# Gates and turned projections of a two-block fp32 kernel as one 512-column product, its bank halves added by ScalarE and VectorE

## The chip, the cores and the metric

The kernel runs on one core of one Trainium2 chip. The metric is the device time of one execution in microseconds (us): the median of several executions. TensorE (PE in the profile) multiplies, VectorE (DVE), ScalarE (ACT) and GpSimd (POOL) do the rest, and SyncE (SP) issues the transfers. Each engine takes its own instructions strictly in the order in which they were issued, and engines meet only in semaphores.

## What is computed

Two transformer blocks over one sequence of 256 rows of 1024 values, in fp32, each with two layers. What matters here is the middle of a layer, cut from the reference of block 2 (block 1 has the same form with three mixers, gmlp, retention and NSA, and a bias in the gates):

```python
u = rms_norm_2(x, norm_mix_g[layer])
proj = jnp.einsum('bsd,de->bse', u, w_in[layer])
(a_in, bq, bk, bv, cq, ck, cv, co, cgate, dq, dk, dv, gates) = split_cols(proj)
y_a = fourier_mix(a_in)
y_b = gqa_branch(bq, bk, bv, qk_norm_g[layer], cos, sin)
y_c = mlstm_branch(cq, ck, cv, co, cgate, mlstm_gate_bias[layer], mlstm_norm_g[layer])
y_d = diff_branch(dq, dk, dv, diff_lambda[layer], diff_norm_g[layer], rel_bias, layer + 1)
ys = jnp.stack([y_a, y_b, y_c, y_d], axis=2)
branch = jnp.einsum('bsnc,ncd->bsnd', ys, w_branch[layer])
g = jax.nn.sigmoid(gates.reshape(b, s, N_BRANCHES, D_MODEL))
merged = jnp.sum(g * branch, axis=2)
x = x + merged @ w_out[layer]
```

Around the middles stand the feed-forward parts (two in a layer of block 1, one with a convolution in a layer of block 2).

## The kernel before

**Precision.** Every fp32 product is three products of rounded parts: hi by hi, hi by lo, lo by hi (`three_passes`, L394 to L396). The normalised input lies turned (features on the partitions) in two tiles, `hT_hi` and `hT_lo`, of 8 chunks (`KC`, index `c`) of 128 partitions by 256 columns.

**Weights.** They stream through a ring of five slots, in tiles of 128 x 2048 values: SP loads a slot, ACT makes its hi part (`hi_to`, L198), DVE its lo part (`lo_to`, L206), and PE uses it and signals it free. A tile of a middle holds 256 output features, that is two halves of 128.

**The middles.** `Fill` (L670 to L831) holds the projections, gates and branch products of a middle as a list of *units*, each half a tile and mostly 24 matmuls of 256 columns. A mixer takes some of them at fixed places of its own code (`f.tensor(pe, n)`), so that PE has work while the mixer's DVE or ACT steps run, and sets a named mark there; ACT and DVE catch up with the units at places of theirs (`f.scalar(act, name)`, `f.vector(dve, name)`). Units are numbered here from 0 in each middle, as u20 for the unit with index 20. Roles: "N" is a projection with the tokens on the partitions, "T" and "half" a turned one (features on the partitions), "gate" a gate half, "branch" a branch product. Turned ones are in Middle1 `uT`, `rqT`, `rkT`, `kcvcT` (u20, u21), `nqT` (u22 to u25) and `kskwT` (u28, u29), 16 halves in all beside 24 gate halves; in Middle2 `aT`, `gt`, `cqT`, `ckT`, `dqT`, `dkT`, 21 halves beside 32 gate halves.

**Banks.** Units are collected in *groups*: one for a whole projection tile (its two halves stand side by side in the bank), one for each gate half or branch half. Group g uses PSUM bank 6 + g % 2, and its first product waits until group g - 2 is read. Before the change ACT reads projections and gates (`activate`, with Copy, Gelu, Silu or Tanh straight from the bank), and DVE only the branch products (`combine`). After the last half of a tile ACT issues the hi part of the tile five ahead, DVE the lo part of the tile four ahead.

**Order.** All orders are fixed in the code; nothing is scheduled at run time. What follows a unit on DVE is what the mixer's code puts there: in the retention mixer (`Retention.vector`, lines before L1082) DVE does the statistics and layer norm of `a_ret_y` (L1061 to L1079) and only then `f.vector(dve, "ret_y")`, the catching up with u22 to u25. PE meanwhile does these four units (L1041), then transposes `a_ret_y` (L642).

Of the kernel before, what the change touches and what calls it, by code (L numbers as in the profile page):

```python
# [9 lines left out]
F32R = mybir.dt.float32r  # L10
# [113 lines left out]
class Core:  # L124


    def __init__(self, nc, ctx):
# [5 lines left out]
        self.hT_hi = sb("hT_hi", [P, KC, SEQ], F32R)  # L133
        self.hT_lo = sb("hT_lo", [P, KC, SEQ], F32R)
# [535 lines left out]
class Fill:  # L670
# [3 lines left out]

    def __init__(self, k, ph, n0, norm, roles, branches, half_bias, gate, mix, ys):
# [21 lines left out]
        self.units[1:3] = self.units[2:0:-1]  # L697
        self.act_out, self.dve_out, self.gated, self.taken, self.mixed = (ph.sem(n) for n in (
            "f_act_out", "f_dve_out", "f_gated", "f_taken", "f_mixed"))
        self.tmp = ph.sb("f_tmp", [P, 2, SEQ])  # L700
        self.out_of, self.mix_at, self.gate_at, self.proj_out = {}, {}, {}, {}
        counts = {"act": 0, "dve": 0, "gate": 0, "taken": 0, "mix": 0}
        sems = {"act": self.act_out, "dve": self.dve_out, "gate": self.gated, "taken": self.taken, "mix": self.mixed}
        for u, (n, h, last, group, role) in enumerate(self.units):
            if not last and role[0] not in ("gate", "branch"):
                continue
# [45 lines left out]
    def product(self, pe, u):  # L752
# [1879 lines left out]
```

## Time and profile before

| | |
|---|---|
| time before, median of 3 runs | 2455.48 us (2451.62 to 2455.94) |
| the profiled execution: its own time | 2453.13 us |
| its span in the trace | 2451.4 us |
| PE busy | 2414.5 us, 98% |
| DVE busy | 1392.6 us, 57% |
| ACT busy | 1138.8 us, 46% |

The share is of the span. The span is the stretch between the first and the last recorded instruction; 1.7 us of the execution lie around it. The profile is of one execution, so differences are made against its own time.

### The profile page before, as it was taken

What the parts mean: (1) busy time and instruction counts of PE and PEld (TensorE: products, weight loads), DVE (VectorE), ACT (ScalarE), POOL (GpSimd) and SP (SyncE); (2) the same over time, 40 slices, a digit from 0 to 9 for tenths busy, and PEclk for the clock granted to TensorE, in tenths of its full rate; (3) what the DMA queues carried; (4) which work ended last, traced back from release to release, by engine and by line L of the source; (5) the groups of instructions that cost most, each with busy time, mean ns of one, the idle gap of its engine ahead of it and who ended that gap; (6) DMA issues with size and microseconds to landing.
All of it is one profiled execution on the core that took longest, in us unless ns stands there. A gap on an engine that the chain in (4) does not pass through costs nothing.

```text
span 2451.4 us, 40355 instructions
## 1 busy us (share of the span) xinstructions
PE 2414.5 (98%) x17632; PEld 2270.4 (93%) x17632; DVE 1392.6 (57%) x1724; ACT 1138.8 (46%) x1591; POOL 62.1 (3%) x110
## 2 busy tenths in 40 slices
PE   8999999999999999999999999999999999999998
PEld 7999999999999999999999899999999999999998
DVE  4546555555454466465544645586655645586665
ACT  5445445454354453454544444354545444355543
POOL 0000000000000000000000100000000100000000
PEclk9999999999999999999999999999999999999999
DMA  6564533455545545334554443344554443344553
GB/s 244 190 214 174 194 126 116 155 176 186 189 172 186 207 168 193 130 112 170 207 185 176 155 138 121 121 155 172 180 190 172 156 154 129 121 146 172 191 183 117
DMA packets 60255, 407.15 MB, mean 166 GB/s; under 512 B 7696, under 2 KB 9232, under 8 KB 12464
## 3 DMA queue, kind: packets, MB, share of 16 engines
q1 hardware_dynamic: 60080, 404.58, 46.5%
q8 instruction: 139, 2.28, 0.4%
q14 instruction: 36, 0.29, 0.0%
HBM read 401.93 MB, written 2.10 MB: 165 GB/s over the span
## 4 chain that ended last, share of the span: by engine, by line
PE 90%; DVE 4%; ACT 2%; DMA 1%; issue 1%; POOL 1%; SPq 0%; POOLq 0%; DVEq 0%; ACTq 0%
PE bank L394 27%; PE bank L396 26%; PE bank L395 26%; DVE w_lo L206 2%; DMA w_raw<-in_tiles 1%; DVE hT_lo L342 1%; PE bank L1821 1%; PE bank L1593 1%; PE bank L1312 1%; PE bank L1233 1%; PE bank L1824 1%; PE bank L1304 1%; PE bank L1445 1%; PE bank L1612 1%; PE bank L1303 1%
## 5 line engine op out<-in xcount | busy, mean ns | idle before, releaser
L394 PE MATMUL bank<-hT_hi,w_hi 128*128 128x256 f32 x3408 | 974.3, 286 | 2.2 <-ACT b_dv L805 1.3
L396 PE MATMUL bank<-hT_hi,w_lo 128*128 128x256 f32 x3408 | 966.2, 284 | 0.0
L395 PE MATMUL bank<-hT_lo,w_hi 128*128 128x256 f32 x3408 | 966.2, 284 | 0.0
L206 DVE TENSOR_TENSOR w_lo<-w_raw,w_hi 128x2048 fp32r<-128x2048 f32 x370 | 843.2, 2285 | 97.3 <-ACT w_hi L198 97.0
L198 ACT ACTIVATE w_hi<-w_raw 128x2048 fp32r<-128x2048 f32 x370 | 705.3, 1909 | 187.3 <-DMA w_raw<-in_tiles 187.0
L394 PEld LDWEIGHTS bank<-hT_hi,w_hi 128*128 128x128 f32 x3408 | 655.3, 192 | 7.5 <-issue 1.9
L395 PEld LDWEIGHTS bank<-hT_lo,w_hi 128*128 128x128 f32 x3408 | 655.2, 192 | 2.6
L396 PEld LDWEIGHTS bank<-hT_hi,w_lo 128*128 128x128 f32 x3408 | 654.9, 192 | 0.0
L615 DVE TENSOR_TENSOR a_ffn_g<-a_ffn_act,bank 128x256 f32<-128x256 f32 x88 | 37.0, 421 | 340.0 <-ACT a_ffn_act L567 339.9
L394 PE MATMUL bank<-w_hi,hT_hi 128*128 128x256 f32 (+1 forms) x736 | 215.2, 292 | 12.9 <-DVE hT_lo L342 10.0
L395 PE MATMUL bank<-w_lo,hT_hi 128*128 128x256 f32 (+1 forms) x736 | 211.1, 287 | 0.0
L396 PE MATMUL bank<-w_hi,hT_lo 128*128 128x256 f32 (+1 forms) x736 | 211.1, 287 | 0.0
L567 ACT ACTIVATE a_ffn_act<-bank 128x256 f32<-128x256 f32 x88 | 33.9, 385 | 295.8 <-PE bank L396 284.3
L394 PEld LDWEIGHTS bank<-w_hi,hT_hi 128*128 128x128 f32 x736 | 145.1, 197 | 20.5 <-issue 11.1
L395 PEld LDWEIGHTS bank<-w_lo,hT_hi 128*128 128x128 f32 x736 | 145.4, 198 | 0.1
L396 PEld LDWEIGHTS bank<-w_hi,hT_lo 128*128 128x128 f32 x736 | 145.0, 197 | 0.0
L394 PE MATMUL bank<-w_hi,a_ffn_g_hi 128*128 128x512 f32 x352 | 140.3, 399 | 0.0
L395 PE MATMUL bank<-w_lo,a_ffn_g_hi 128*128 128x512 f32 x352 | 139.7, 397 | 0.0
L396 PE MATMUL bank<-w_hi,a_ffn_g_lo 128*128 128x512 f32 x352 | 139.6, 397 | 0.0
L607 DVE SCALAR_TENSOR_TENSOR b_ffn_conv<-bank,cols,b_ffn_conv 128x255 f32<-128x255 f32 x44 | 21.2, 482 | 107.1 <-ACT b_ffn_conv L572 107.0
L396 PEld LDWEIGHTS bank<-w_hi,a_ffn_g_lo 128*128 128x128 f32 x352 | 66.5, 189 | 16.2
L800 ACT ACTIVATE b_gate<-bank 128x256 f32<-128x256 f32 x64 | 24.4, 384 | 120.7 <-PE bank L396 120.7
(332 smaller groups left out, 2934.1 us busy)
## 6 DMA issues: line engine op xcount, KB each, us to landing
w_raw<-in_tiles SPq DMA_DIRECT2D x370, 1024.0 KB, 4.8
a_cmp_w<-in_cmp_w SPq DMA_DIRECT2D x2, 2048.0 KB, 8.3
a_gm_rows<-in_rows SPq DMA_DIRECT2D x2, 768.0 KB, 6.8
x_res<-in_x SPq DMA_DIRECT2D x2, 512.0 KB, 4.8
rel_line<-a_line SPq DMA_DIRECT2D x1, 1024.0 KB, 9.1
a_ret_rows<-in_rows SPq DMA_DIRECT2D x2, 512.0 KB, 8.2
b_rows<-in_rows SPq DMA_DIRECT2D x2, 512.0 KB, 6.6
out<-x_res SPq DMA_DIRECT2D x4, 256.0 KB, 2.0
```

Source lines behind the costliest of these rows:

```text
L198: act.activation(k.hi[slot][:], k.raw[slot][:], ACT.Copy).then_inc(k.hi_done[slot], 1)
L206: dve.tensor_tensor(k.lo[slot][:], k.raw[slot][:], k.hi[slot][:].bitcast(F32), ALU.subtract).then_inc(k.lo_done[slot], 1)
L342: dve.scalar_tensor_tensor(out=k.hT_lo[:, c, ts], in0=self.turned(t, c), scalar=self.gain[:, c:c + 1], in1=k.hT_hi[:, c, ts].bitcast(F32), ...
L394: pe.matmul(out, w[0], x[0], start=start, stop=False)
L395: pe.matmul(out, w[0], x[1], start=False, stop=False)
L396: return pe.matmul(out, w[1], x[0], start=False, stop=stop)
L567: act.activation(self.s1[j][:], a[:, 0:SEQ], ACT.Silu).then_inc(self.act_done[j], 1)
L615: dve.tensor_tensor(self.g[j][:], self.s1[j][:], a[:, SEQ:2 * SEQ], ALU.mult).then_inc(self.g_done[j], 1)
L1233: last = pe.matmul(k.bank[i][:, 0:32], self.w1[:, i, j], self.win[i][:, j].rearrange("p g n -> p (g n)"), start=(j == 0), stop=(j == 15))
L1303: pe.matmul(b[:, 0:P], self.qT[r, h % 4, 0:P], self.kskwT[r, u // NSA_H, 0:P], start=True, stop=True)
L1304: pe.matmul(b[:, P:SPAN], self.qT[r, h % 4, P:SEQ], self.kskwT[r, u // NSA_H, :], start=True, stop=True).then_inc(self.qk_mm, 1)
L1312: last = pe.transpose(k.bank[2 + u % 2][:, j * P:(j + 1) * P], pr[u % 2][:, j * P:(j + 1) * P], k.ident[:])
```

## The change

`hT_hi` and `hT_lo` become one tile, `hT[P, KC, 2, SEQ]`, in which chunk c of hi and lo lie side by side. Gates, "T" and "half" units are computed by a new function, `with_both`: for each c one matmul of 512 columns with w's hi part (hi by hi into the bank's lower half, hi by lo into the upper one), and one of 256 columns with w's lo part, accumulated on the upper half. So a unit is 16 matmuls where it was 24, and fills a whole bank. Each half of a "T" tile is therefore a group of its own. ACT copies the upper half of the bank to the destination (semaphore `f_part`), DVE adds the lower half to it (`f_dve_out`), and where a Gelu or a Tanh is due, ACT applies it afterwards in place (`finish`). PE's wait for the bank is now for DVE's add. The ring's signals follow (`HALVES1`, `HALVES2`). Projections of role "N", the branch products, the output product and the feed-forward parts stay as they are.

```diff
-        self.hT_hi = sb("hT_hi", [P, KC, SEQ], F32R)
-        self.hT_lo = sb("hT_lo", [P, KC, SEQ], F32R)
+        self.hT = sb("hT", [P, KC, 2, SEQ], F32R)
+        self.hT_hi, self.hT_lo = self.hT[:, :, 0], self.hT[:, :, 1]
...
+def with_both(pe, k, slot, half, bank):
+
+    for c in range(KC):
+        at = c * 256 + half * P
+        pe.matmul(bank[:], k.hi[slot][:, at:at + P], k.hT[:, c].rearrange("p a s -> p (a s)"), start=c == 0, stop=False)
+        last = pe.matmul(bank[:, SEQ:2 * SEQ], k.lo[slot][:, at:at + P], k.hT_hi[:, c], start=False, stop=c == KC - 1)
     return last
...
         for role in roles:
             halves = 1 if role[0] == "half" else 2
-            self.units += [(n0, h, h == halves - 1, group, role) for h in range(halves)]
-            group += 1
+            for h in range(halves):
+                self.units.append((n0, h, h == halves - 1, group, role))
+                group += role[0] == "T"
+            group += role[0] != "T"
             n0 += 1
...
     def scalar_to(self, act, upto):
+        before = None
         for u in range(self.at["act"], upto):
             self.activate(act, u)
+            if before is not None:
+                self.finish(act, before)
+            before = u if u in self.part_at else None
+        if before is not None:
+            self.finish(act, before)
         self.at["act"] = max(self.at["act"], upto)
...
-        if group - 2 in self.out_of and (half == 0 or role[0] in ("gate", "branch")):
+        if group - 2 in self.out_of and (half == 0 or role[0] in ("T", "gate", "branch")):
             pe.wait_ge(*self.out_of[group - 2])
-        if role[0] == "gate":
-            features_major(pe, k, slot, half, bank[:, 0:SEQ]).then_inc(k.used[slot], 1)
+        if u in self.part_at:
+            with_both(pe, k, slot, half, bank).then_inc(k.used[slot], 1)
...
-            bias = self.half_bias[:, b * KC + c:b * KC + c + 1] if self.half_bias is not None else 0.0
-            act.activation(self.gate[:, c], self.bank(group)[:, 0:SEQ], ACT.Tanh, bias=bias,
-                           scale=0.5).then_inc(self.gated, 1)
+            scale = role[1][1] if role[0] != "gate" and role[1][0] == ACT.Copy else 1.0
+            act.activation(self.whole(u), self.bank(group)[:, SEQ:2 * SEQ], ACT.Copy, scale=scale).then_inc(self.part, 1)
...
+    def finish(self, act, u):
+        n, half, last_half, group, role = self.units[u]
+        out = self.whole(u)
+        if role[0] == "gate":
+            b, c = role[1:]
+            act.wait_ge(self.dve_out, self.sum_at[u])
+            bias = self.half_bias[:, b * KC + c:b * KC + c + 1] if self.half_bias is not None else 0.0
+            act.activation(out, out, ACT.Tanh, bias=bias, scale=0.5).then_inc(self.gated, 1)
+        elif role[1][0] != ACT.Copy:
+            act.wait_ge(self.dve_out, self.sum_at[u])
+            act.activation(out, out, role[1][0], scale=role[1][1]).then_inc(self.act_out, 1)
...
+        if u in self.part_at:
+            dve.wait_ge(self.part, self.part_at[u])
+            out, scale = self.whole(u), role[1][1] if role[0] != "gate" and role[1][0] == ACT.Copy else 1.0
+            if scale == 1.0:
+                dve.tensor_tensor(out, self.bank(group)[:, 0:SEQ], out, ALU.add).then_inc(self.dve_out, 1)
+            else:
+                dve.scalar_tensor_tensor(out=out, in0=self.bank(group)[:, 0:SEQ], scalar=scale, in1=out, op0=ALU.mult,
+                                         op1=ALU.add).then_inc(self.dve_out, 1)
```

What that does to the order is shown at two places. The first is the retention mixer of Middle1. DVE before, from the lo part issued ahead of the statistics to the lo parts behind the layer norm (`a_ret_y`); a row is line, operation, out<-in, size and the semaphores that it waits for:

```order
L206 TENSOR_TENSOR w_lo_55<-w_raw_50,w_hi 128x2048 [waits w_hi_done1]
L1061 BN_STATS a_ret_st<-bank 128x6 [waits a_ret_pv_ok,a_ret_rows_in]
...
L1079 TENSOR_TENSOR a_ret_y<-a_ret_y,a_rg 128x1024 [waits a_f_act_out,a_ret_chain]
L206 TENSOR_TENSOR w_lo_56<-w_raw_51,w_hi 128x2048 [waits w_hi_done2]
L206 TENSOR_TENSOR w_lo_57<-w_raw_52,w_hi 128x2048 [waits w_hi_done3]
L657 TENSOR_TENSOR a_y_lo<-bank,a_y_hi 128x256 [waits a_ret_hi_done] x4
```

Two adds for u20 and u21 now stand ahead of that lo part, and the adds for u22 to u25 behind the layer norm. DVE now, the same stretch:

```order
L863 TENSOR_TENSOR a_kcvcT<-bank,a_kcvcT 128x256 [waits a_f_part] x2
L206 TENSOR_TENSOR w_lo_55<-w_raw_50,w_hi 128x2048 [waits w_hi_done1]
L1116 BN_STATS a_ret_st<-bank 128x6 [waits a_ret_pv_ok,a_ret_rows_in]
...
L1134 TENSOR_TENSOR a_ret_y<-a_ret_y,a_rg 128x1024 [waits a_f_act_out,a_ret_chain]
L865 SCALAR_TENSOR_TENSOR a_nqT<-bank,a_nqT 128x256 [waits a_f_part] x2
L206 TENSOR_TENSOR w_lo_56<-w_raw_51,w_hi 128x2048 [waits w_hi_done2]
L865 SCALAR_TENSOR_TENSOR a_nqT<-bank,a_nqT 128x256 [waits a_f_part] x2
L206 TENSOR_TENSOR w_lo_57<-w_raw_52,w_hi 128x2048 [waits w_hi_done3]
L666 TENSOR_TENSOR a_y_lo<-bank,a_y_hi 128x256 [waits a_ret_hi_done] x4
```

The queue gained six adds, two of them ahead of the chain that ends at `a_ret_y` and four behind it. PE before, from u22 to the transposes of `a_ret_y`; each unit is 24 rows of which the first two or three are shown:

```order
L394 MATMUL bank<-hT_hi,w_hi 128x256 [waits a_f_act_out,w_lo_done4]
L395 MATMUL bank<-hT_lo,w_hi 128x256
L396 MATMUL bank<-hT_hi,w_lo_58 128x256
...
L394 MATMUL bank<-hT_hi,w_hi 128x256 [waits a_f_act_out,w_lo_done0]
L395 MATMUL bank<-hT_lo,w_hi 128x256
L396 MATMUL bank<-hT_hi,w_lo_54 128x256
...
L642 MATMUL bank<-ident,a_ret_y 128x128 [waits a_ret_y_ok]
```

PE now, the same stretch, where each unit is 8 pairs of rows:

```order
L428 MATMUL bank<-hT,w_hi 128x512 [waits a_f_dve_out,w_lo_done4]
L429 MATMUL bank<-hT,w_lo_58 128x256
...
L428 MATMUL bank<-hT,w_hi 128x512 [waits a_f_dve_out]
L429 MATMUL bank<-hT,w_lo_58 128x256
...
L428 MATMUL bank<-hT,w_hi 128x512 [waits a_f_dve_out,w_lo_done0]
L429 MATMUL bank<-hT,w_lo_54 128x256
...
L428 MATMUL bank<-hT,w_hi 128x512 [waits a_f_dve_out]
L429 MATMUL bank<-hT,w_lo_54 128x256
...
L651 MATMUL bank<-ident,a_ret_y 128x128 [waits a_ret_y_ok]
```

All four units wait for DVE's adds, each for that of the unit two ahead, where two waits for ACT stood. The second place is the start of Middle2, DVE: before, the norm of the queries of the gqa mixer (`b_gqa_qn`) with the lo parts around it:

```order
L206 TENSOR_TENSOR w_lo_58<-w_raw_53,w_hi 128x2048 [waits w_hi_done4]
L1533 TENSOR_TENSOR b_gqa_qn<-b_qkv,b_gqa_rs 128x640 [waits b_gqa_rooted]
...
L1539 TENSOR_TENSOR b_gqa_qn<-b_gqa_qn,b_rows_150 128x128
L206 TENSOR_TENSOR w_lo_54<-w_raw_49,w_hi 128x2048 [waits w_hi_done0,b_gqa_chain]
L1545 TENSOR_TENSOR b_gqa_sq<-b_gqa_qn,b_rope_sin 128x10x32
```

And DVE now:

```order
L863 TENSOR_TENSOR b_aT<-bank,b_aT 128x256 [waits b_f_part] x2
L206 TENSOR_TENSOR w_lo_58<-w_raw_53,w_hi 128x2048 [waits w_hi_done4]
L1588 TENSOR_TENSOR b_gqa_qn<-b_qkv,b_gqa_rs 128x640 [waits b_gqa_rooted]
...
L1594 TENSOR_TENSOR b_gqa_qn<-b_gqa_qn,b_rows_150 128x128
L863 TENSOR_TENSOR b_aT<-bank,b_aT 128x256 [waits b_f_part,b_gqa_chain]
L863 TENSOR_TENSOR b_aT<-bank,b_aT 128x256 [waits b_f_part]
L206 TENSOR_TENSOR w_lo_54<-w_raw_49,w_hi 128x2048 [waits w_hi_done0]
L1600 TENSOR_TENSOR b_gqa_sq<-b_gqa_qn,b_rope_sin 128x10x32
```

The adds for `aT`'s first half tiles (u6, u7) came ahead of the norm, those for u8 and u9 behind it.

## Rows read from the trace of the kernel before

**Rows 1.** Page, busy time of each engine, share of the span, instructions.
```profile
PE 2414.5 (98%) x17632; PEld 2270.4 (93%) x17632; DVE 1392.6 (57%) x1724; ACT 1138.8 (46%) x1591; POOL 62.1 (3%) x110
```

**Rows 2.** Waits of PE: releaser, us in total, times, longest us.
```profile
PE bank L394 <- DVE hT_lo L342: 10.0, 11, 1.3
```

**Rows 3.** Timeline, PE, 99.9 to 107.2 us: start, duration, line, matmul.
```profile
100.17 0.40 PE L394 MATMUL bank<-w_hi,a_ffn_g_hi 128*128 128x512 f32 x1
...
105.77 0.28 PE L394 MATMUL bank<-hT_hi,w_hi 128*128 128x256 f32 x1
...
106.83 0.28 PE L394 MATMUL bank<-hT_hi,w_hi 128*128 128x256 f32 x1
...
107.19 0.28 PE L394 MATMUL bank<-hT_hi,w_hi 128*128 128x256 f32 x1
```

**Rows 4.** Page, groups: count, busy us, mean ns, idle before.
```profile
L206 DVE TENSOR_TENSOR w_lo<-w_raw,w_hi 128x2048 fp32r<-128x2048 f32 x370 | 843.2, 2285 | 97.3 <-ACT w_hi L198 97.0
...
L615 DVE TENSOR_TENSOR a_ffn_g<-a_ffn_act,bank 128x256 f32<-128x256 f32 x88 | 37.0, 421 | 340.0 <-ACT a_ffn_act L567 339.9
...
L800 ACT ACTIVATE b_gate<-bank 128x256 f32<-128x256 f32 x64 | 24.4, 384 | 120.7 <-PE bank L396 120.7
```

**Rows 5.** Timeline, DVE, 230.5 to 248 us (gmlp).
```profile
233.18 1.42 DVE L940 BATCH_NORM_STATS2 a_gm_st<-a_v 128x6 f32<-128x512 f32 x2
...
240.75 1.29 DVE L951 TENSOR_TENSOR a_v<-a_v,a_gm_rows 128x512 f32<-128x512 f32 x2
```

**Rows 6.** Timeline, PE, 228.5 to 229.2 us (start of u4).
```profile
229.02 0.28 PE L394 MATMUL bank<-hT_hi,w_hi 128*128 128x256 f32 x1
```

**Rows 7.** Timeline, DVE, 281 to 303.2 us (retention).
```profile
283.92 2.29 DVE L206 TENSOR_TENSOR w_lo<-w_raw,w_hi 128x2048 fp32r<-128x2048 f32 x1 [1.02 <-ACT w_hi L198]
289.68 1.68 DVE L1061 BATCH_NORM_STATS2 a_ret_st<-bank 128x6 f32<-128x128 f32 x8 [3.47 <-PE bank L1025]
...
299.53 1.23 DVE L1079 TENSOR_TENSOR a_ret_y<-a_ret_y,a_rg 128x1024 f32<-128x1024 f32 x1
```

**Rows 8.** Timeline, PE, 288.6 to 302 us (u22, the transposes, u26).
```profile
289.33 0.37 PE L394 MATMUL bank<-hT_hi,w_hi 128*128 128x256 f32 x1
...
300.93 1.04 PE L642 MATMUL bank<-ident,a_ret_y 128*128 128x128 f32 x8
301.72 0.26 PE L394 MATMUL bank<-w_hi,hT_hi 128*128 128x32 f32 x1
```

**Rows 9.** Stretches (`kskwT`): PE, PEld, DVE, ACT, POOL busy (count), granted clock, DMA.
```profile
310.00:315.00 5.00, 5.00 (x26) 5.00 (x26) 3.26 (x5) 1.71 (x1) 0.00 (x0) 0.53 0.56 210
```

**Rows 10.** Timeline, DVE, 311 to 338.8 us (compressed keys).
```profile
313.95 0.62 DVE L1157 TENSOR_TENSOR a_cmp_win<-a_kcvcT,a_cmp_pos 64x120 f32<-64x120 f32 x2
...
318.11 0.63 DVE L1157 TENSOR_TENSOR a_cmp_win<-a_kcvcT,a_cmp_pos 64x120 f32<-64x120 f32 x2
...
331.77 0.28 DVE L1168 COPY a_cmp_hid<-a_cmp_hid 128x256 f32<-128x256 f32 x1
```

**Rows 11.** Timeline, PE, 318 to 322 and 335 to 338 us.
```profile
320.48 1.75 PE L1233 MATMUL bank<-a_cmp_win,a_cmp_w 128*128 128x32 f32 x15
...
336.43 0.61 PE L1243 MATMUL bank<-a_cmp_w,a_cmp_hid 128*128 128x64 f32 x4
```

**Rows 12.** Timeline, PE, 1390 to 1398 us (Fourier's first product, after u10).
```profile
1393.26 3.61 PE L1434 MATMUL bank<-b_dft_feat,b_aT 128*128 128x256 f32 x16
```

**Rows 13.** Timeline, DVE, 1384 to 1599 us (Middle2), five ends of mixer steps.
```profile
1391.76 1.70 DVE L1539 TENSOR_TENSOR b_gqa_qn<-b_gqa_qn,b_rows 128x512 f32<-128x512 f32 x4
...
1402.63 2.48 DVE L1461 COPY b_four_m<-bank 128x512 f32<-128x512 f32 x4
...
1467.56 0.69 DVE L1561 COPY b_gqa_pT<-bank 128x512 f32<-128x512 f32 x1 [4.60 <-PE bank L1603]
...
1513.71 0.68 DVE L1707 TENSOR_TENSOR b_ml_F<-b_ml_F,b_ml_M 4x512 f32<-4x512 f32 x1
...
1595.56 1.22 DVE L1765 SCALAR_TENSOR_TENSOR b_ml_y<-b_og,b_ml_y 128x1024 f32<-128x1024 f32 x1
```

More of the change, by code:

```diff
@@ L697, in __init__ @@
         self.units[1:3] = self.units[2:0:-1]
+        self.part = ph.sem("f_part")
         self.act_out, self.dve_out, self.gated, self.taken, self.mixed = (ph.sem(n) for n in (
@@ L704, in __init__ @@
         for u, (n, h, last, group, role) in enumerate(self.units):
-            if not last and role[0] not in ("gate", "branch"):
+            if role[0] in ("T", "half", "gate"):
+                self.part_at[u] = len(self.part_at) + 1
+                counts["dve"] += 1
+                self.sum_at[u] = counts["dve"]
+                self.out_of[group] = (self.dve_out, counts["dve"])
+                if role[0] == "gate":
+                    counts["gate"] += 1
+                    self.gate_at[u] = counts["gate"]
+                elif role[1][0] == ACT.Copy:
+                    self.proj_out[n] = self.out_of[group]
+                else:
+                    counts["act"] += 1
+                    self.proj_out[n] = (self.act_out, counts["act"])
+                continue
+            if not last and role[0] != "branch":
                 continue
@@ L807, in activate, with whole @@
             k.ring.hi_to(act, n + SLOTS)
+    def whole(self, u):
+        n, half, last_half, group, role = self.units[u]
+        if role[0] == "gate":
+            return self.gate[:, role[2]]
+        return role[2][:, half] if role[0] == "T" else role[2]
+    def finish(self, act, u):
+        n, half, last_half, group, role = self.units[u]
+        out = self.whole(u)
+        if role[0] == "gate":
+            b, c = role[1:]
+            act.wait_ge(self.dve_out, self.sum_at[u])
[4 more added lines that the diff above has]
+            act.activation(out, out, role[1][0], scale=role[1][1]).then_inc(self.act_out, 1)
     def combine(self, dve, u):
@@ L826, in combine @@
                 dve.tensor_tensor(mix, mix, self.tmp[:], ALU.add).then_inc(self.mixed, 1)
-        elif role[0] != "gate" and last_half and role[3] == "dve":
+        elif last_half and role[3] == "dve":
             k.ring.wait_used(dve, n, 1)
@@ L2313, in program @@
             at1.append((ring.add(ffn_places(base + F1_AT), FFN_SIGNALS),
-                        ring.add(list(range(base + PROJ1_AT, base + F2_AT)), middle_signals(PROJ1_TILES, BRANCHES1)),
+                        ring.add(list(range(base + PROJ1_AT, base + F2_AT)), middle_signals(HALVES1, BRANCHES1)),
                         ring.add(ffn_places(base + F2_AT), FFN_SIGNALS)))
@@ L2317, in program @@
             base = BLOCK2_AT + l * STREAM2
-            at2.append((ring.add(list(range(base + PROJ2_AT, base + UP_AT)), middle_signals(PROJ2_TILES, BRANCHES2)),
+            at2.append((ring.add(list(range(base + PROJ2_AT, base + UP_AT)), middle_signals(HALVES2, BRANCHES2)),
                         ring.add(ffn_places(base + UP_AT), FFN_SIGNALS)))
```

28 lines of the change are left out of this document (13 added, 15 removed).

## The prediction, made before the changed kernel was run

> **What bounds the kernel now.** The page first: PE is busy for 2414.5 of 2451.4 us, DVE for 57%, ACT for 46% [rows 1]. PE's waits come next: the largest is 10.0 us in eleven pieces for `hT_lo`, at the start of a stage [rows 2]. So the time is PE's own work, product behind product, and a change counts in two ways only: by what a product costs PE, and by what makes PE wait. Then the timelines of DVE at the places where `Fill`'s units lie beside a mixer's steps, since PE's release of a bank moves from ACT to DVE. I read them in program order beside PE's timeline, and the two orders tell which step of DVE stands ahead of which add.
>
> **Fewer products.** Middle1 has 16 turned halves and 24 gate halves in a layer, Middle2 21 and 32: (40 + 53) x 2 layers = 186 units, x 8 chunks = 1488 steps. In each, three matmuls of 256 columns become one of 512 and one of 256. PE starts a 256-column one every 120 ns (three in 107.19 - 106.83 us), and a 512-column one every 233 ns (24 in 105.77 - 100.17 us) [rows 3]. Right behind 512s, nine of 256 took 106.83 - 105.77 us, 118 ns each. So a step goes from 360 ns to 233 + 117 to 120 = 350 to 353, which saves about 10 ns. If the 256 paid its 120 and the 512 were at the slow end (236 ns), it would be 4; if a 256 behind a 512 hid some of its start, up to 19, a bound I set as the double of the middle, since no row shows the two in turn. 1488 x 10 ns = 14.9 us gained, 6 to 28 as the ends. The duration in the groups isn't used, since matmuls overlap.
>
> The Trainium skill (page TensorE: Matmul & The Clock Gate, section Back-to-back issue gap) gives the distance of two isolated matmuls at full clock as columns / 2.4 plus about 2.5 ns: by that a step would go from 327.5 to 324.9 ns, and the 1488 would gain 3.9 us where I take 14.9. The starts 120 and 233 ns apart [rows 3] differ from it in both sizes, and the rows decide the sum; a rival below holds that small gain.
>
> **The adds themselves.** ACT's copy of a half costs 0.38 us like the gate's, DVE's add 0.42 us like L615 [rows 4]. 186 adds are 78 us more on DVE, 1393 + 78 = 60% of the span, and ACT gets some 40 us: no bound by sum. Beside PE's unit of 16 matmuls (8 x 0.352 = 2.8 us) they are hidden, as long as DVE is free. A group's bank is wanted again two units later, so between the end of unit u and the start of u + 2 lie 2.8 us; copy and add take 0.8 of them, and 2.0 are slack. Where DVE stands in a step of a mixer for longer than that, PE waits. Before, ACT alone read these banks, which is why the same DVE steps cost nothing. The lo part (2.29 us [rows 4]) is ahead of some adds too. Behind PE's wait everything is queued that follows it, the mixer's own matmuls among them.
>
> **Middle1, per layer.** In gmlp u4 starts at 229.02 [rows 6], u6 two units of 2.91 us later, at 234.8 (234.6 with the saving). It waits for add(4), which stands behind the statistics of `a_v` (from 233.18 [rows 5], with their two aggregates to 235.0): 235.4, so 0.8 us. u8 at 241.2 waits for add(6) behind the norm that ends at 240.75 + 1.29 = 242.04: 242.5, so 1.3 us.
>
> Retention is the large one. By then PE is 1.3 us late in all, so u21 ends at about 290.2, its copy and add at 291.05. The lo part, which ran early at 283.92, now stands behind that add: to 293.35. The chain from the statistics to `a_ret_y` took from 289.68 to 299.53 + 1.23 = 300.76, 11.08 us [rows 7], part of it a round to POOL; it ends at 304.4, add(22) at 304.85. PE has begun u22 at 289.33 + 1.3 = 290.6 [rows 8], needs 5.6 us for u22 and u23, and stands before u24 at 296.2: **8.7 us** (6.4 if the lo part doesn't come in between). What was covered before by four units, with the transposes at 300.93 [rows 8] just behind `a_ret_y`, is now covered by two. u24, u25 and the transposes follow only then.
>
> After such a gap I expect TensorE's clock to be at its lower level (1.2 of 2.4 GHz) for a while. In this trace the granted clock is 0.53 at 310 to 315, behind the short transposes (300.93) and 48 products of only 32 columns that begin at 301.72 [rows 8], so the engine was fully fed there, but with narrow work. Those 5 us hold 26 products of `kskwT` [rows 9]; at 120 ns they are 3.1 us, so five such microseconds lose **1.9 us**. I add that once, at this stall alone.
>
> The windows of the compressed keys (L1157, sixteen operations from 313.95 to 318.7 [rows 10]) get add(28), add(29) and a lo part ahead of them: u29 ends 2.9 us before 320.48 [rows 11], at 317.8 with its overlap; 0.8 + 2.3 + half of the sixteen, 2.3, give 323.2, and PE's L1233 was due at 320.5: 2.7 us. The copy at L1168 (331.77 [rows 10]) gets add(32), add(33) and a lo part ahead of it: 336.4 + 0.8 + 2.3 + 0.3 = 339.8, and L1243 was due at 336.43 [rows 11]: 3.4 us. Sum: 0.8 + 1.3 + 8.7 + 1.9 + 2.7 + 3.4 = 18.8, x 2 layers = **37.6 us**.
>
> **Middle2, per layer.** u10 is reached at 1390.2 (one unit before 1393.26 [rows 12]) and waits for add(8) behind the norm of the queries, 1391.76 + 1.70 + 0.42 = 1393.9 [rows 13]: 3.7. u13 waits for add(11) behind the four copies at 1402.63 (which have moved too): 1.0. At four steps of gqa an add stands behind the copy `b_gqa_pT` (1467.56 + 0.69 + 0.42 = 1468.7, where PE would begin at 1468.1): 4 x 0.55 = 2.2. u42 waits for add(40) behind the scans of mlstm (to 1514.39, so 1514.8; PE would be there at 1513.4): 1.4. u60 waits for add(58) behind `b_ml_y` (1595.56 + 1.22 + 0.42 = 1597.2 against 1596.0): 1.2. At the like places of the differential mixer I put 1.6, an estimate from the last two. Sum 11.1, x 2 = **22.2 us**. In NSA's steps, in the tail of the differential mixer and in the output product the adds have room of 1 us or more and cost nothing; if DVE's extra 0.42 per unit uses that room up, it is up to 1 us a mixer, at most some 6 us in all.
>
> **What is hidden.** `finish` puts Gelu and Tanh behind the add; the branch product that uses a gate comes at least one unit later, and ACT is half idle: nothing. SP's loads wait for the same last half as before: nothing. The second signal of a turned tile is free on PE.
>
> **Sum.** 2453.1 - 14.9 + 37.6 + 22.2 = 2498.0 us against the profiled execution; that lay 2.35 us below the median of the runs, so against the median 2455.5 + 44.9 = **2500 us**, with 2488 to 2513 for this case alone (6.4 for 8.7, gain 6 to 28).
>
> **The rivals.** *The adds are never in the way.* ACT hands over early, DVE is at 57%, and PE waits no longer than now. That needs each add to be done within 2.0 us of its copy. For it: the average; against it: the rows of the chain, in which DVE is taken for 11.08 us by steps that stand ahead of add(22) in its order. It gives 2455.5 - 14.9 = 2441, faster. 7%.
>
> *Only the long chain holds, and the product gains at its better end.* The short waits (under 1.5 us and those where I placed a lo part in between) vanish because DVE runs earlier than I placed it. Then 2 x (6.4 + 1.9 + 3.4 + 3.7) = 30.8, less 14.9 to 28: 2458 to 2471, or some 2480 where half of the others stay. Slower, 16%.
>
> *The clock falls at more stalls.* Gaps of 2.7 to 3.7 us might be enough; there are three in a pair of layers, so six in all, each with 1.9 us behind it: 2500 + 11 = 2511, and the four places of gqa and the small ones may add to 2514, up to 2520 with NSA's room used up. The rows show the lower clock behind narrow work, not behind a gap, so what a gap does is open. 13%.
>
> *The product gains next to nothing.* If a 256 behind a 512 pays more of its start than a 256 behind a 256, a step falls by 2.6 ns only (inside the bounds above, near their low end of 4), so that two kinds of start cost more than three alike. The sum is then 11 us higher, 2511. The rows at 118 ns behind 512s speak against it. It is the gain that the rule of the Trainium skill cited above gives. 6%.
>
> **How the numbers follow.** The forecast has 58%, the others 7, 16, 13 and 6. The range takes in the short-chain case from its upper half and the clock's up to its upper end: 2474 to 2520. A measurement of this kernel can tell 0.2%, 5 us, from no change. Faster by more: the first rival, 7%, and 1% of the second; same: 4% of the second, at its lower end; slower the rest, 88%.
>
> **What would show it.** Pairs of L428 and L429 starting 350 to 353 ns apart at full clock. PE's waits: `a_nqT` L865 as the releaser, twice, about 8.7 us each; L1233 and L1243 waiting for L1212 and the copy behind it, 2.7 and 3.4 us; `b_aT` L863 3.7 us. The granted clock near 0.5 right behind the retention stall. PE's waits would add to some 55 us more than before. I am wrong if the waits for `a_f_dve_out` sum to under 20 us, or if a pair takes under 341 or over 358 ns.

## The result and the profile after

| | before | after |
|---|---|---|
| median of four executions | 2453.55 us (2450.34 to 2455.94) | 2509.67 us (2506.74 to 2512.23) |
| ratio | | 1.0234 (95% interval 1.0221 to 1.0247), slower |
| span of the profiled execution | 2451.4 us | 2509.9 us |
| its mean granted TensorE clock | 0.990 | 0.981 |

The change made the kernel 56 us slower by the medians, where 45 us more was forecast: 2500 us, with 2474 to 2520 as the range. The page of the changed kernel, busy time, and under it the groups of the new product and the waits of PE (releaser, us in total, times, longest):

```profile
PE 2426.1 (97%) x16144; PEld 2203.7 (88%) x16144; DVE 1458.9 (58%) x1910; ACT 1180.5 (47%) x1747; POOL 54.1 (2%) x110
...
L428 PE MATMUL bank<-hT,w_hi 128*128 128x512 f32 x1488 | 545.8, 408 | 32.5 <-DVE a_nqT L865 16.4
...
L429 PE MATMUL bank<-hT,w_lo 128*128 128x256 f32 x1488 | 421.3, 283 | 0.0
```

```profile
PE bank L428 <- DVE a_nqT L865: 16.4, 2, 8.2
PE bank L394 <- DVE hT L342: 9.9, 11, 1.3
PE bank L1298 <- DVE a_cmp_hid L1223: 6.3, 2, 3.2
...
PE bank L428 <- DVE b_gate L863: 5.2, 4, 1.6
PE bank L1288 <- DVE a_cmp_win L1212: 5.0, 2, 2.5
PE bank L428 <- DVE b_aT L863: 3.2, 2, 1.6
PE bank L428 <- DVE a_uT L863: 3.2, 4, 0.9
...
PE bank L2067 <- DVE b_z_lo L666: 1.7, 2, 0.9
PE bank L428 <- DVE b_dqT L863: 1.5, 4, 0.4
```

There are 1488 fewer matmuls (17632 in [rows 1], 16144 now), and yet PE is busy for 12 us more: the busy time isn't the sum of the products' work, it also takes in slower starts at the lower clock. `hT`, the largest wait before [rows 2], is unchanged; all the large new ones are for DVE, and all are at places that the prediction named. With the smaller ones they add up to some 45 us.

Where the time went by stage. A stage runs here from the first product behind a norm to that of the next, read from the starts in the two traces, in us:

| | before | after | forecast of the difference |
|---|---|---|---|
| Middle1, first layer | 279.6 | 301.0 | +15.6 |
| Middle1, second layer | 281.1 | 301.1 | +15.6 |
| Middle2, first layer | 350.3 | 360.5 | +6.9 |
| Middle2, second layer | 348.9 | 355.7 | +6.9 |
| the feed-forward stages between | 777.2 | 776.7 | 0 |

The middles hold all of it, +58.5, and each middle of block 1 is 4 to 6 us beyond its forecast.

The stall in retention, where PE waits before u24. PE's timeline, then DVE's of the same stretch:

```profile
297.11 0.40 PE L428 MATMUL bank<-hT,w_hi 128*128 128x512 f32 x1
297.34 0.28 PE L429 MATMUL bank<-hT,w_lo 128*128 128x256 f32 x1
...
305.84 0.77 PE L428 MATMUL bank<-hT,w_hi 128*128 128x512 f32 x1 [8.22 <-DVE a_nqT L865]
```

```profile
291.76 0.42 DVE L863 TENSOR_TENSOR a_kcvcT<-bank,a_kcvcT 128x256 f32<-128x256 f32 x1 [2.41 <-ACT a_kcvcT L829]
292.10 2.28 DVE L206 TENSOR_TENSOR w_lo<-w_raw,w_hi 128x2048 fp32r<-128x2048 f32 x1
294.30 1.68 DVE L1116 BATCH_NORM_STATS2 a_ret_st<-bank 128x6 f32<-128x128 f32 x8
...
304.13 1.23 DVE L1134 TENSOR_TENSOR a_ret_y<-a_ret_y,a_rg 128x1024 f32<-128x1024 f32 x1
305.27 0.75 DVE L865 SCALAR_TENSOR_TENSOR a_nqT<-bank,a_nqT 128x256 f32<-128x256 f32 x2
```

Add, lo part, the chain from the statistics to `a_ret_y` (294.30 to 305.36, 11.06 us as in [rows 7]), and only then the add that PE waits for. That is the forecast's sequence step by step, less than a microsecond later. ACT's timeline of the same stretch has something that the forecast didn't:

```profile
298.54 1.91 ACT L198 ACTIVATE w_hi<-w_raw 128x2048 fp32r<-128x2048 f32 x1 [6.81 <-DMA w_raw<-in_tiles]
300.36 0.64 ACT L829 ACTIVATE a_nqT<-bank 128x256 f32<-128x256 f32 x2
```

u22 was finished near 294.7, but ACT copied its upper half only at 300.36: in its order a hi part stands ahead of the copy, and that one waited for a weight tile to land. The copy is done before DVE comes to its add, so it cost nothing here. It becomes the next wait as soon as DVE is quicker (below). The same lateness was there before the change, and cost nothing either:

```profile
297.12 1.92 ACT L198 ACTIVATE w_hi<-w_raw 128x2048 fp32r<-128x2048 f32 x1 [7.57 <-DMA w_raw<-in_tiles]
298.94 0.58 ACT L805 ACTIVATE a_nqT<-bank 128x512 f32<-128x512 f32 x1
```

The granted clock behind the stalls; columns as in [rows 9]:

```profile
298.00:306.00 8.00, 0.16 (x1) 0.20 (x2) 7.10 (x16) 4.37 (x4) 2.29 (x5) 0.60 0.63 254
306.00:310.00 4.00, 4.00 (x13) 3.42 (x14) 2.22 (x2) 0.00 (x0) 0.09 (x1) 0.51 0.00 0
310.00:316.00 6.00, 6.00 (x46) 5.58 (x45) 2.47 (x3) 2.85 (x5) 0.00 (x0) 1.00 0.20 67
316.00:322.00 6.00, 6.00 (x33) 6.00 (x33) 4.10 (x6) 0.82 (x3) 0.00 (x0) 0.56 0.27 111
...
336.00:340.00 4.00, 4.00 (x26) 4.00 (x26) 3.94 (x8) 0.00 (x0) 0.00 (x0) 0.65 0.00 0
340.00:344.00 4.00, 4.00 (x20) 4.00 (x20) 0.05 (x1) 0.20 (x1) 0.00 (x0) 0.50 0.02 4
344.00:354.00 10.00, 10.00 (x74) 9.35 (x73) 0.42 (x1) 2.98 (x4) 0.00 (x0) 1.00 0.32 105
356.00:362.00 6.00, 4.27 (x17) 3.80 (x18) 3.20 (x8) 1.01 (x2) 0.00 (x0) 0.72 0.39 162
```

In the stall itself (298 to 306) the clock falls, and PE then works for 4 us at its lower level, 13 matmuls; half of 4 us is 2 us lost, where 1.9 was forecast. The stretch at 316 is like the one that stood at 304.5 to 314.7 in the trace of before (its second half is in [rows 9]). New in this layer are 336 to 344 and 356 to 362, each right behind one of the two waits of the compressed keys: 0.35 x 4, 0.50 x 4 and 0.28 x 6 are 5.1 us lost there. Over the whole execution the mean clock fell from 0.990 to 0.981, 0.009 x 2510 = 23 us of lowered clock more, some 6 us of it inside the retention waits.

### The profile page after: what moved, and what is told of

It is laid out like the page before. It is cut to its first block, busy times and chain, and to the rows that moved or that the text cites. A ratio compares the mean times of both kernels' runs of the same rounds, so it can differ in the third digit from the quotient of the medians.

```text
span 2509.9 us, 37721 instructions
## 1 busy us (share of the span) xinstructions
PE 2426.1 (97%) x16144; PEld 2203.7 (88%) x16144; DVE 1458.9 (58%) x1910; ACT 1180.5 (47%) x1747; POOL 54.1 (2%) x110
## 4 chain that ended last, share of the span: by engine, by line
PE 82%; DVE 10%; ACT 3%; issue 2%; DMA 2%; POOL 1%; SPq 0%; POOLq 0%; DVEq 0%; ACTq 0%
PE bank L394 19%; PE bank L396 18%; PE bank L395 18%; PE bank L428 11%; PE bank L429 6%; DVE w_lo L206 4%; DMA w_raw<-in_tiles 2%; DVE hT L342 1%; ACT w_hi L198 1%; PE bank L1288 1%; PE bank L1876 1%; PE bank L1648 1%; PE bank L1367 1%; PE bank L1879 1%; PE bank L1359 1%
## 5 line engine op out<-in xcount | busy, mean ns | idle before, releaser
L428 PE MATMUL bank<-hT,w_hi 128*128 128x512 f32 x1488 | 545.8, 408 | 32.5 <-DVE a_nqT L865 16.4
L394 PE MATMUL bank<-hT,w_hi 128*128 128x256 f32 x1920 | 543.6, 283 | 0.0
L396 PE MATMUL bank<-hT,w_lo 128*128 128x256 f32 x1920 | 543.0, 283 | 0.0
L395 PE MATMUL bank<-hT,w_hi 128*128 128x256 f32 x1920 | 542.8, 283 | 0.0
L429 PE MATMUL bank<-hT,w_lo 128*128 128x256 f32 x1488 | 421.3, 283 | 0.0
L428 PEld LDWEIGHTS bank<-hT,w_hi 128*128 128x128 f32 x1488 | 285.3, 192 | 104.1 <-issue 31.8
L394 PEld LDWEIGHTS bank<-hT,w_hi 128*128 128x128 f32 x1920 | 367.2, 191 | 3.0 <-DVE w_lo L206 0.8
L395 PEld LDWEIGHTS bank<-hT,w_hi 128*128 128x128 f32 x1920 | 367.1, 191 | 2.4
L396 PEld LDWEIGHTS bank<-hT,w_lo 128*128 128x128 f32 x1920 | 367.2, 191 | 0.0
L429 PEld LDWEIGHTS bank<-hT,w_lo 128*128 128x128 f32 x1488 | 286.7, 193 | 0.2
L394 PE MATMUL bank<-w_hi,hT 128*128 128x256 f32 (+1 forms) x736 | 217.2, 295 | 14.7 <-DVE hT L342 9.9
L396 PE MATMUL bank<-w_hi,hT 128*128 128x256 f32 (+1 forms) x736 | 212.9, 289 | 0.0
L395 PE MATMUL bank<-w_lo,hT 128*128 128x256 f32 (+1 forms) x736 | 212.9, 289 | 0.0
L394 PEld LDWEIGHTS bank<-w_hi,hT 128*128 128x128 f32 x736 | 147.2, 200 | 23.1 <-issue 13.2
L395 PEld LDWEIGHTS bank<-w_lo,hT 128*128 128x128 f32 x736 | 147.2, 200 | 0.0
L396 PEld LDWEIGHTS bank<-w_hi,hT 128*128 128x128 f32 x736 | 147.1, 200 | 0.0
```

Source lines behind the costliest of these rows:

```text
L394: pe.matmul(out, w[0], x[0], start=start, stop=False)
L395: pe.matmul(out, w[0], x[1], start=False, stop=False)
L396: return pe.matmul(out, w[1], x[0], start=False, stop=stop)
L428: pe.matmul(bank[:], k.hi[slot][:, at:at + P], k.hT[:, c].rearrange("p a s -> p (a s)"), start=c == 0, stop=False)
L429: last = pe.matmul(bank[:, SEQ:2 * SEQ], k.lo[slot][:, at:at + P], k.hT_hi[:, c], start=False, stop=c == KC - 1)
```

## The experiments

All ratios are to the kernel before, run beside each kernel on the same chip, where it took 2452.1 to 2452.6 us.

**The product by itself.** Two kernels take the change apart: one keeps the copies and adds and undoes the 512-column product. The other keeps the product and leaves the adds out: ACT alone reads the bank, its lower half, and releases it.

```diff
-        pe.matmul(bank[:], k.hi[slot][:, at:at + P], k.hT[:, c].rearrange("p a s -> p (a s)"), start=c == 0, stop=False)
+        pe.matmul(bank[:, 0:SEQ], k.hi[slot][:, at:at + P], k.hT_hi[:, c], start=c == 0, stop=False)
+        pe.matmul(bank[:, SEQ:2 * SEQ], k.hi[slot][:, at:at + P], k.hT_lo[:, c], start=False, stop=False)
```

> The changed kernel, but the 512-column product of each chunk is split into two of 256 into the same bank halves: 24 matmuls a unit again, while ScalarE's copy, VectorE's add and the release of the bank by that add stay as changed. Theory (the loss is PE waiting for adds that stand behind a mixer's steps on VectorE, and the product itself gains about 10 ns a chunk): the waits stay, the gain goes, 1488 x 9.6 ns = 14 us more than the changed kernel, about 2520 us (the waits shrink a little, since PE arrives later: 2516 to 2524). Rival (the 512-column product itself costs, by more activity of the array and a clock that is lowered more often): the time falls towards the kernel before, below 2500.

Measured: 2518.01 us, ratio 1.026 (1.0239 to 1.0281). The waits stayed where they were (for `a_nqT` 16.2 us, for the copy behind the compressed keys 6.3), and 8 us came on top of the changed kernel's 2509.7, where 14 were expected. The two medians are from different chips, so the difference of the ratios, 0.0026 with 0.0025 to either side, leaves 0.2 to 12 us, and the 14 lie just outside. The rival, that the product itself costs, falls: undoing it made nothing faster.

```diff
-            act.activation(self.whole(u), self.bank(group)[:, SEQ:2 * SEQ], ACT.Copy, scale=scale).then_inc(self.part, 1)
...
+                act.activation(self.whole(u), self.bank(group)[:, 0:SEQ], ACT.Tanh, bias=bias,
+                               scale=0.5).then_inc(self.gated, 1)
+            else:
+                act.activation(self.whole(u), self.bank(group)[:, 0:SEQ], role[1][0],
+                               scale=role[1][1]).then_inc(self.act_out, 1)
...
-            dve.wait_ge(self.part, self.part_at[u])
...
-                dve.tensor_tensor(out, self.bank(group)[:, 0:SEQ], out, ALU.add).then_inc(self.dve_out, 1)
```

> The 512-column products as changed, but the upper half of the bank (w hi by x lo and w lo by x hi) is left out of the result: ScalarE reads only the lower half with Gelu, Tanh or Copy straight from the bank and releases it, VectorE adds nothing. It measures the product by itself. Theory: 1488 chunks gain 9.6 ns each and nothing waits more than before: 14 us below the kernel before, about 2439 us. Rival (the product itself costs, by the clock): 2453 us or more. Rival (the ring's gain only moves PE's wait to the weights): between 2445 and 2453.

Measured: 2452.46 us, ratio 0.9998 (0.9988 to 1.0009), no difference. That is not the theory's 2439. The time lies at the rival's 2453, but not for the rival's reason. Nor does PE wait for weights, the second rival: `w_lo` stands at 2.6 us in its list of waits, as before. The page and PE's waits show what stood against the gain, and the timeline of ACT where it came from:

```profile
PE 2400.8 (98%) x16144; PEld 2185.2 (89%) x16144; DVE 1392.6 (57%) x1724; ACT 1142.7 (47%) x1627; POOL 61.9 (3%) x110
...
PE bank L428 <- ACT a_nqT L823: 7.7, 2, 3.9
```

```profile
288.15 0.38 ACT L823 ACTIVATE a_kcvcT<-bank 128x256 f32<-128x256 f32 x1 [2.45 <-PE bank L429]
295.92 1.91 ACT L198 ACTIVATE w_hi<-w_raw 128x2048 fp32r<-128x2048 f32 x1 [7.39 <-DMA w_raw<-in_tiles]
297.74 0.64 ACT L823 ACTIVATE a_nqT<-bank 128x256 f32<-128x256 f32 x2
```

And SyncE's, where the tile's load is issued behind the transfer of `kcvcT`, which waits for u21:

```profile
288.56 1.16 SPq L1177 DMA_DIRECT2D a_cmp_swap<-a_kcvcT  x2
289.77 5.02 SPq L189 DMA_DIRECT2D w_raw<-in_tiles  x3
```

So even without any add, u24 waits for ACT's copy of u22, which stands behind a hi part, which waits for a load, which waits for u21. Before, one bank held both halves of a tile, so between the end of a group and the reuse of its bank lay a whole tile of 48 matmuls (5.8 us) where now lies one unit of 16 (2.8 us), and the same lateness was covered. Giving every half its own bank has a price of its own: 2 x 3.9 us. Over the pairs of this trace at full clock the starts are 234.5 and 116.6 ns apart, 351 ns a chunk against 3 x 119.8 = 359 in the trace of before: 8.3 ns, or 12.4 us for 1488 chunks. (Left out are some 75 starts in either trace that come 80 ns or more late.) The two pages agree: PE was busy for 13.7 us less than before, and idle for 8.9 more. So do the stages: the middles of block 2, which have no such wait, take 346.7 and 346.8 us where they took 350.3 and 348.9, and those of block 1 280.9 and 281.1 against 279.6 and 281.1. The ten executions had a mean granted clock of 0.9898, those of before 0.9907, 2.2 us more. 12.4 - 7.7 - 2.2 leaves 2.5 us, inside the measured interval (2.9 us faster to 2.2 slower).

**Which part loses: gates or turned projections.**

```diff
-            if role[0] in ("T", "half", "gate"):
+            if role[0] in WIDE:      # WIDE = ("gate",)
```

> Only the gate halves (112 of the 186 units) use the 512-column product and the two-engine sum; the turned projections are as before the change. Theory: the waits of the first part of both middles (retention 8.2, compressed keys 2.5 and 3.1, gmlp 0.9 and 1.0, aT 1.6 us, per layer) vanish with the lowered clock behind them; those at the gates of Middle2 (1.0, 1.9, 1.3 us) stay, about 10 us in both layers with what follows; 896 chunks gain 8.6 us: 2450 to 2460 us. Rival (the loss is spread over all such products, or it is the 512-column product's own): 60% of the 56 us, about 2487.

Measured: 2465.28 us, ratio 1.005 (1.0034 to 1.0067). Most of the loss left with the turned projections (a middle of block 1 takes 284.3 us, not 301.0), which rules out a loss spread over all such products (2487). But it missed the expected 2450 to 2460, by a fault of mine: I had counted the wait at the compressed keys' copy among the turned ones. The adds ahead of it are those of u32 and u33, which are gate halves, and the wait is still there, with lowered clock behind it (third row; the wait ends near 339):

```profile
PE bank L1318 <- DVE a_cmp_hid L1243: 6.3, 2, 3.2
...
PE bank L428 <- DVE b_gate L883: 5.2, 4, 1.6
...
338.00:346.00 8.00, 6.73 (x24) 5.88 (x25) 2.79 (x9) 1.01 (x4) 0.00 (x0) 0.57 0.27 113
```

**The lo part between add and step.**

```diff
+            if last_half:
+                k.ring.lo_to(dve, n + SLOTS - 1)
             dve.wait_ge(self.part, self.part_at[u])
```

> The changed kernel, but VectorE issues the lo part of the weight tile four ahead before the add of a tile's last half, not after it. Nothing else differs. Theory: where a lo part of 2.29 us stood between an add that waits for PE and a mixer's step, it runs earlier, in VectorE's idle time: retention's wait falls from 8.5 to about 6.2, those of the compressed keys from 2.5 and 3.1 us to about 0.5 and 1, so 6 to 7 us a layer of block 1, 13 us in all, and a few more if the clock is lowered less often behind them: 2485 to 2498 us. Rival (the lo part was never on that path): 2510 us as the changed kernel.

Measured: 2513.95 us, ratio 1.0247 (1.0229 to 1.0265), not better than the changed kernel, and outside the expected 2485 to 2498. By stage the theory holds and fails at once: the middles of block 1 fell from 301.0 and 301.1 to 294.1 and 287.9 us, those of block 2 rose from 360.5 and 355.7 to 371.7 and 364.3.

```profile
PE bank L428 <- DVE b_gate L865: 17.3, 8, 3.7
PE bank L428 <- DVE a_nqT L867: 12.4, 2, 6.4
...
PE bank L428 <- DVE b_aT L865: 7.1, 2, 3.6
...
PE bank L428 <- DVE a_uT L865: 3.7, 4, 1.3
```

Where the add is early and a mixer's step is late, the lo part belongs ahead (`a_nqT`: 16.4 to 12.4); where a chain has made the add late already, a lo part ahead of it adds its own 2.29 us to PE's wait (`b_gate`: 5.2 to 17.3, `b_aT`: 3.2 to 7.1). A rule for all places only moved the loss.

**Two chains hold one bank.** Two kernels take retention's wait apart. The first has the lo part ahead in Middle1 alone, and the adds of u22 and u23 inside the norm's chain:

```diff
         last.then_inc(self.var_ok, 1)
+        f.vector(dve, "ret_u22")
         dve.wait_ge(self.rooted, 2)
...
                                      ALU.subtract, ALU.mult)
+        f.combine(dve, f.at["dve"], part_only=True)
         link(last)
```

> The changed kernel with two edits on VectorE in Middle1: a lo part goes ahead of the add of the last half of its tile (in Middle1 alone), and in retention the adds for u22 and u23 are moved up into the norm chain, the first before the wait for GpSimd's root, the second before the first multiplication by the rows. If VectorE's order were all that holds the bank, the wait of 6.3 to 6.7 us left at u24 by the lo part's move alone would be gone. In the traces ScalarE's copies of u22 and u23 start only at 300.0 and 300.2 us, behind a hi part that waits for a weight tile to land (298.1), while PE is at u24 at 297.0. Theory (two chains hold the bank): a wait of about 4 us stays at u24, released by VectorE's add, which itself waits for ScalarE's copy: about 2486 us. Rival (VectorE's order alone): the wait at u24 goes to under 1 us, and the time to about 2478.

The second adds one edit on ACT, the hi part of u21's tile behind the two copies:

```diff
-        if last_half:
+        if last_half and not (u == 21 and len(self.mix_at) == 12):
             k.ring.hi_to(act, n + SLOTS)
```

> The kernel with VectorE's adds early, and one more edit on ScalarE: in Middle1 the hi part that stands behind u21 is issued behind the copies of u22 and u23. Theory (the bank at u24 was held by VectorE's chain and, behind it, by ScalarE's copy waiting for a weight tile that SyncE loads only after the transfer of kcvcT): the copies run as soon as u22 and u23 are done, the wait at u24 and u25 falls to under 1 us, one of 1 to 2 us stays before the transposes of ret_y: 5 us a layer less than with the lo part's move alone, and the lowered clock behind the wait goes too: about 2476 us. Rival (the copy's wait is not on the path): as the kernel with the adds early alone.

Measured: 2488.12 us, ratio 1.0143 (1.0129 to 1.0157), and 2481.79 us, 1.0118 (1.0104 to 1.0132), against 2486 and 2476. With the adds early PE's wait at u24 is still there, up to 4.4 us:

```profile
PE bank L428 <- DVE a_nqT L868: 8.2, 2, 4.4
```

With the copies first it is gone, since they run as soon as their unit is done, ahead of the hi part that waits for its load. ACT's timeline:

```profile
293.45 0.38 ACT L829 ACTIVATE a_nqT<-bank 128x256 f32<-128x256 f32 x1 [3.10 <-PE bank L429]
296.28 0.38 ACT L829 ACTIVATE a_nqT<-bank 128x256 f32<-128x256 f32 x1 [2.45 <-PE bank L429]
297.13 1.92 ACT L198 ACTIVATE w_hi<-w_raw 128x2048 fp32r<-128x2048 f32 x1 [0.47 <-DMA w_raw<-in_tiles]
```

A smaller one came in its place, since the two copies left behind came late themselves:

```profile
PE bank L394 <- DVE a_nqT L868: 3.1, 2, 1.5
...
PE bank L651 <- DVE a_ret_y L1142: 0.5, 1, 0.5
```

So both rivals that named one engine fall. DVE's chain held the bank for the last 4 us, and behind it stood ACT's copy. The middles of block 1 are down to 285.8 and 285.5 us with this kernel, 31 us less than in the changed one; that takes in what the lo part ahead of the adds saves at the compressed keys. The 6 us above its expectation aren't assigned: a wait of 1 to 2 us before the transposes was expected, and the trace has 0.5 once there and 1.5 a layer at the tile behind them.

**What a wait of 3 us costs beyond itself.** Only u28, u29, u32 and u33 of Middle1 are undone, those ahead of the compressed keys' two steps; all others stay as changed.

```diff
-            if role[0] in ("T", "half", "gate"):
+            if u in self.wide:      # all turned and gate halves but 28, 29, 32, 33 of Middle1
```

> The changed kernel with only four units of a Middle1 layer undone (kskwT's u28 and u29, and the gate halves u32 and u33, whose adds stood ahead of the compressed keys' windows and of the copy behind them); 178 of 186 units stay as changed. The two waits were 2.5 and 3.1 us by the profile. Theory (a wait of this size also lowers TensorE's clock behind it, as rows of the changed kernel show granted clock near half at 336 to 344 and 356 to 362 us): a layer of block 1 gets shorter by more than the two waits, by 8 to 11 us, and the kernel falls to about 2490 us. Rival (the lowered clock there would come anyway, and only the waits go): 5.7 us a layer less, 0.6 of it given back by the four units, so about 2499 us.

Measured: 2486.12 us, ratio 1.0137 (1.0123 to 1.0151). Two waits of 2.5 and 3.2 us a layer, 11.3 us in both layers, went, and the kernel is 23.6 us faster than the changed one (by the two ratios' intervals, 19 to 28). The rival's 2499 is ruled out. The stages fell by 10.4 and 12.8 us. The clock, same stretches as above:

```profile
336.00:340.00 4.00, 4.00 (x36) 4.00 (x36) 0.00 (x0) 1.24 (x3) 0.00 (x0) 1.00 0.16 20
340.00:344.00 4.00, 4.00 (x37) 4.00 (x36) 2.50 (x2) 1.54 (x2) 0.00 (x0) 1.00 0.60 246
344.00:354.00 10.00, 10.00 (x73) 9.35 (x72) 1.95 (x7) 3.13 (x4) 0.00 (x0) 1.00 0.30 107
```

No lowered clock is left at 336 to 344 in this layer. In the first layer the fall is 5.7 us of waits and the 5.1 us of clock behind them. In the second it is 5.6 of waits, 3.4 of clock behind them, and 5.1 of clock that the changed kernel had lost ahead of the windows, where the two kernels are the same. So a wait of about 3 us cost between one and a half times and twice its length.

The two waits aren't equally clear. Each of the six waits of 3.2 us in the traces (of the changed kernel, of that with the split product and of that with gates alone, two layers each) has lowered clock beginning within 1 us of its end, and none of the other eight traces has any at that place. Among the products of the windows, where the wait of 2.5 us stood, the clock is lowered in places without that wait too, in the kernel before for one:

```profile
984.00:998.00 14.00, 14.00 (x97) 14.00 (x97) 3.43 (x3) 2.79 (x4) 0.00 (x0) 0.76 0.24 86
```

So part of the 336 to 344 stretch may come without the wait; no run separates it.

**The product where DVE is free.** If waits for adds are the price, the product should pay where no step of a mixer stands ahead of the add. The same selection, other numbers: u8 to u11 and all gate halves but the first two in Middle1, u13 to u18 and 20 of the 32 gate halves in Middle2, 104 units of 186.

> The 512-column product with the two-engine sum only at 104 of the 186 units, those whose add did not stand behind a mixer's steps: per layer of block 1 the turned units u8 to u11 and all gate halves but the first two, per layer of block 2 u13 to u18 and 20 of the 32 gate halves. All others as before the change. Theory: 104 x 8 chunks gain 9.6 ns each, 8.0 us, and no new wait stands against it: 0.33% faster than the kernel before, about 2444 us. Rival (adds and copies cost wherever they are, as small delays of the steps around them): the gain is eaten, 2450 to 2456 us.

> The same kernel as the one with the product only where VectorE is free, run once more, since its ratio of 0.9988 had an interval of 0.9977 to 0.9999. Theory (the product gains 104 x 8 chunks x 7.1 ns = 5.9 us by the starts in its trace, the mixers' own matmuls lose 2.3 us by small delays, and the rest is the clock, which differs from execution to execution): 3 to 4 us faster at an equal mean granted clock, 2448 to 2450 us against 2452. Rival (no gain at all): 2452 us, a ratio of 1.000.

Measured: 2450.86 us, ratio 0.9988 (0.9977 to 0.9999), then 2448.72 us, 0.9982 (0.9973 to 0.9991). The first missed its 2444 and lies where its rival had put it; the second agrees with its theory, which was made from the first. It is the one kernel that beats the one before, by 0.12% and 0.18%, 2 to 4 us. No wait for an add is left among PE's largest:

```profile
PE bank L394 <- DVE hT L342: 9.9, 11, 1.3
...
PE bank L394 <- ACT b_dv L856: 1.3, 2, 0.6
PE bank L394 <- ACT b_gate L851: 0.9, 2, 0.5
```

The first expectation of 8.0 us took 9.6 ns a chunk; the trace has 352.3 ns against 359.4, 5.9 us for 832 chunks. The mixers' own matmuls take 2 to 3 us longer in sum; by the starts in both traces that is not a small delay of each, as the expectation had it, but lies wholly in stretches of lowered clock. The rest is noise of a kind that can be named: executions of one kernel differ with their mean granted clock. Of 43 executions of before the 15 at a clock of 0.992 averaged 2449.5 us, the 13 at 0.990 took 2453.4, the two at 0.988 took 2458.4. Of the 22 of this kernel those at the same three values took 2444.8, 2449.7 and 2454.2. At an equal clock it is 3.7 to 4.7 us faster.

## Why the prediction was right

**Direction, place and mechanism: right.** The waits are where the sum had them. In us a layer, forecast and then as the profile has it: retention 8.7 and 8.2; compressed keys 2.7 and 2.5; the copy behind them 3.4 and 3.2; gmlp's two together 2.1 and 1.6; u10 3.7 and 1.6; u13 1.0 and 0.5; the steps of gqa 2.2 and 1.5; u42 and u60 together 2.6 and 2.6; the differential mixer 1.6 and about 2, of which the list shows 0.9. Sum of the two layers: 56 forecast without the clock, some 45 by the list of waits. The largest miss is u10: PE reaches it 24.8 us after the stage's start where it took 23.1 before, with a stretch of lowered clock in between (0.63 at 1408 to 1412), while the norm that it waits for, itself held by a result of POOL, ends 25.8 us after it (26.2 before).

**The product: right, slightly too large.** 10 ns a chunk was forecast from the two kinds of start, each by itself; 8.3 ns was measured in the kernel without adds, 12.4 us instead of 14.9. The working's own 350 to 353 ns give 7 to 10, and the sum took the upper end; 351 was measured, in the changed kernel too. The 118 ns behind 512s [rows 3] was the right row to use (116.6 measured). The rule cited from the Trainium skill (page TensorE: Matmul & The Clock Gate, section Back-to-back issue gap) is for isolated matmuls, and gives 2.5 ns a step, 3.7 us in all (the prediction's 2.6 and 3.9 are a slip in rounding); the 8.3 ns measured here don't agree with it.

**The clock: the term that was mis-sized.** The sum had 1.9 us once a layer of block 1. That was right for the place that it named (2.0 at 306 to 310) and missed the others. The rival "the clock falls at more stalls", held at 13%, is half of what happened: the clock is lowered behind the waits of 2.5 and 3.2 us too, and the kernel with four units undone puts the price of that at 8.5 us in the two layers by the stretches behind the waits, 12 by the totals. Waits came out 11 us smaller than forecast and the clock some 13 us larger (17 outside the stalls, where 3.8 were forecast), so the total owes its nearness in part to luck, two misses of opposite sign. The difference itself, 56 us, is a quarter more than the 45 forecast.

**The bounds.** The 2488 to 2513 given for the forecast's own case don't follow from its terms: 6.4 for 8.7 in two layers and a gain of 28 make 2482, a gain of 6 makes 2509. The wider range didn't rest on them.

**A step that was missing.** The working looked at DVE alone for the release of a bank, and took ACT's copy as 0.38 us after the product. In retention it came 5.7 us late, behind a hi part waiting for its load. The time of the changed kernel was not wrong by it, since DVE was later still; but it named only the first of two chains that hold the bank, and a repair on DVE alone leaves 4 of the 8 us, as the kernel with the adds early shows.

**What stays open.** Span less busy time says that PE was idle for 36.9 us before and 83.8 now, 47 us more, which the listed waits explain almost wholly. With -12.4 for the product and 17 for the clock (23 less what falls into the stalls) that makes 51 of the 58.5 us of span, or 54 where the lowered stretches of the two traces are summed instead of the rounded means taken. The 4 to 7 us that are left lie in PE's busy time, not in waits; no run assigned them.

## What to carry to other kernels

When a buffer's release moves to another engine, walk that engine's order, not its busy share: DVE was busy for 57% and still stood 11 us in one chain ahead of an add of 0.42 us. Then walk the second engine that has to come first as well, down to the load that its queue head waits for, because the longest chain hides the next. And a change that saves 2% of a product's issue time pays only where nothing new waits: the same edit was 2.3% slower everywhere and 0.12 and 0.18% faster in two runs at the places chosen by the trace.

## What the runs showed of the hardware

A matmul of 256 columns with its own weights starts 119.8 ns after the one before in a stream of its kind, and 116.6 ns after one of 512 columns, which takes 233 to 235: merging two 256s into one 512 saves 8.3 of 359 ns, about 2%, at full clock. At the lower of the two levels it saves nothing: a pair takes 427 + 213 = 640 ns (307 to 309 us in the changed kernel), three 256s take 3 x 213 (310 to 314 us in the one before).

A gap of about 3 us between products costs more than its length. Behind each of six gaps of 3.2 us the granted clock fell to its lower level for some microseconds (0.72 at 356 to 362 us in the changed kernel, 0.57 at 338 to 346 in that with gates alone). Removing gaps of 2.5 and 3.2 us a layer brought back 23.6 us for 11.3 us of waiting; 8.5 of the rest is clock right behind the gaps, and some of that may be the narrow products' own.

Executions of the kernel before took 2447.5 to 2458.7 us, and their mean granted clock orders them: about 2 us for each 0.001 of it. Comparing executions at an equal mean clock made a difference of 4 us visible that the medians of eleven executions each only just showed.
